# Splitting the expert biases on 128 partitions, and both last out projections ahead of turning and routing

## The reference

```
proj = x @ w_in
  [0:256]      causal pooling, windows 2, 4, 8, 16
  [256:1408]   q, k, v of 6 heads x 64, dilated sliding windows, ALiBi
  [1408:2176]  gate * a -> causal depthwise conv of 31 taps -> LN -> swish
mix = concat(pool, attention, conv) @ w_o
x   = LN(alpha*x + mix)
x   = LN(alpha*x + MoE(x))
MoE: logits = x @ router_w + router_b; top 4 of 32 experts, softmax over the four
     hh = x @ e_w_in[e] + e_b_in[e]; gate, up = split(hh)
     act = min(gate,7) * sigmoid(1.702*gate) * (clip(up,-7,7) + 1)
     y  += gate_weight * (act @ e_w_out[e] + e_b_out[e])
```

## Time and profile before

| | before |
|---|---|
| median of 3 runs | 1374.19 us |
| profiled execution | 1375.13 us, span 1373.2 us |
| mean granted TensorE clock | 0.945 |
| PE, DVE, ACT, POOL busy | 1185.9, 533.3, 272.9, 281.9 us |
| DMA | 463.14 MB, mean 337 GB/s |

### The profile page before, as it was taken

How to read it: one execution, slowest core, us unless ns; L and a number is a source line. 1 busy time by engine, 2 the same in 40 slices (tenths; PEclk the granted TensorE clock), 3 DMA queues, 4 the chain that set the end, 5 groups by cost and what they waited for, 6 DMA issues and landing times.

```text
span 1373.2 us, 34108 instructions
## 1 busy us (share of the span) xinstructions
PE 1185.9 (86%) x12516; PEld 532.6 (39%) x12517; DVE 533.3 (39%) x866; ACT 272.9 (20%) x533; POOL 281.9 (21%) x242
## 2 busy tenths in 40 slices
PE   8688999855899999999989999998998989987860
PEld 7577555431333343343233333342333332532220
DVE  3997846653422231324222222222314220432226
ACT  0001333311102221132121212130121211131123
POOL 5900000222121221112211141023121212130113
PEclk9889999957999999999999999999999999998975
DMA  9700680355999999999999999999999999999953
GB/s 335 219 3 0 240 283 33 123 216 204 417 413 411 412 411 413 415 404 406 415 418 410 415 401 413 410 416 402 415 408 414 410 419 393 392 404 419 410 221 126
DMA packets 78828, 463.14 MB, mean 337 GB/s; under 512 B 11908, under 2 KB 19689, under 8 KB 28493
## 3 DMA queue, kind: packets, MB, share of 16 engines
q1 hardware_dynamic: 67931, 438.16, 78.5%
q0 software_dynamic: 8800, 18.26, 5.2%
q10 hardware_dynamic: 2066, 6.32, 1.3%
HBM read 448.29 MB, written 19.48 MB: 341 GB/s over the span
## 4 chain that ended last, share of the span: by engine, by line
PE 54%; DMA 17%; issue 3%; DVE 2%; ACT 0%; SPq 0%; ACTq 0%; DVEq 0%; POOLq 0%; POOL 0%
PE pu L1812 34%; PE rest L1826 18%; DMA ring<-in_e_in 10%; DMA ring<-in_e_out 7%; PE pu L1806 1%; PE rest L1837 1%; DVE fin L2028 0%; DVE bn L2010 0%; DVE xgT L1949 0%; DVE mv L2021 0%; DMA acc_rows<-y,row 0%; DMA fin<-acc_rows 0%; PE rest L1831 0%; ACT y L1892 0%; DMA xq<-x_rows,idx 0%
## 5 line engine op out<-in xcount | busy, mean ns | idle before, releaser
L1812 PE MATMUL pu<-ring,xgT 128*32 128x512 f32 x5248 | 589.6, 601 | 35.3 <-DMA ring<-in_e_in 34.5
L1812 PEld LDWEIGHTS pu<-ring,xgT 128*32 128x32 f32 x5248 | 168.0, 111 | 439.8 <-issue 432.8
L1826 PE MATMUL rest<-ring,hid 128*32 128x256 f32 x5248 | 299.0, 385 | 16.9 <-DMA ring<-in_e_out 11.7
L1979 DVE TENSOR_SCALAR gg<-pu 128x1280 f32<-128x1280 f32 x32 | 47.7, 1492 | 603.6 <-PE pu L1812 603.6
L1735 POOL DMA_INDIRECT acc_rows<-y,row x82 | 110.3, 1346 | 778.4 <-ACT y L1892 737.6
L1826 PEld LDWEIGHTS rest<-ring,hid 128*32 128x32 f32 x5248 | 168.6, 111 | 137.5 <-issue 35.1
L1892 ACT ACTIVATE y<-rest,gate 32x256 f32 x328 | 153.1, 467 | 287.1 <-issue 275.2
L1872 ACT ACTIVATE ss<-gg 128x1280 f32<-128x1280 f32 x32 | 40.7, 1272 | 544.8 <-DVE gg L1979 544.8
L867 PE MATMUL pair<-xt,ring 128*128 128x260 f32 x448 | 104.2, 396 | 20.4 <-DVE conv L1189 14.9
L867 PEld LDWEIGHTS pair<-xt,ring 128*128 128x128 f32 x448 | 88.3, 198 | 35.2 <-DVE conv L1189 15.7
L1725 POOL DMA_INDIRECT xq<-x_rows,idx x82 | 88.3, 1076 | 58.7 <-issue 46.8
(11 more groups left out here) (263 smaller groups left out, 589.7 us busy)
## 6 DMA issues: line engine op xcount, KB each, us to landing
ring<-in_e_in SPq DMA_DIRECT2D x256, 1024.0 KB, 23.1
ring<-in_e_out SPq DMA_DIRECT2D x128, 1024.0 KB, 24.5
ring<-in_w_in SPq DMA_DIRECT2D x3, 1536.0 KB, 30.0
ring<-in_w_in SPq DMA_DIRECT2D x5, 512.0 KB, 9.2
ring<-in_w_o SPq DMA_DIRECT2D x1, 2048.0 KB, 11.9
conv<-in_x_prompt SPq DMA_DIRECT2D x1, 2048.0 KB, 13.8
x_rows<-conv ACTq DMA_DIRECT2D x4, 512.0 KB
acc_rows<-conv ACTq DMA_DIRECT2D x4, 512.0 KB
```

Of the source, the lines that this page charges most:

```text
L1812: mm = nc.tensor.matmul(pu[quarter(c), j], xgT[:, j, k], w[:, :, c * QC:(c + 1) * QC], start=False, stop=k == KT - 1, skip_group_check=True)
L1826: mm = nc.tensor.matmul(py[quarter(c), j], hid[:, j, 2 * q + f], w[:, f, c * QC:(c + 1) * QC], start=False, stop=q == FT // 2 - 1 and f == ...
L1979: V.tensor_scalar(gg[:, :, :], pu[:, :, 0], SW_LIMIT, None, ALU.min).then_inc(g_ready, 1)
```

## The change

The biases are loaded once. Each of the four column quarters goes to one band of 32 partitions of `btok`, 768 columns wide (512 of gate and up, 256 of the out bias), so that 128 partitions are used. GpSimd casts and subtracts in whole: three casts, two subtractions. The three parts then stand in `parts`, in the place of the values, and 24 transfers of SyncE (4 quarters x 3 parts, one for `brow` and one for `drow` each) bring them to their partitions. The loads no longer wait for the input. SyncE waits for the split ahead of the transfers, ScalarE for the transfers (`bias_rows`) where it waited for `brow_ready`, VectorE for the split alone where it waited for `drow_ready`.

In the attention's end, `ln1(1)` moves from step 11 to step 12 (`NORM_AT`), `turn_rows1(1)` and `logits(1)` from the steps 12 and 13 to behind `out_rest(0)`, and `route(1)` behind `ln1(0)`.

```
-TURN_AT = {3: 6, 2: 9, 1: 12}
-LOGITS_AT = {3: 7, 2: 10, 1: 13}
+TURN_AT = {3: 6, 2: 9}
+LOGITS_AT = {3: 7, 2: 10}
+NORM_AT = {3: 5, 2: 8, 1: 12}
...
-        btok = qkv[:, 6 * R:]
-        otok = mix[:, 6:8, :].rearrange("p a r -> p (a r)")[:, 0:D]
+        btok = mix[:, 6:8, :].rearrange("p a r -> p (a r)")[:, 0:3 * QC]
+        parts = qkv[:, 6 * R:6 * R + 9 * QC // 2].bitcast(BF16).rearrange("p (k n) -> p k n", k=3)
...
+            sp.wait_ge(split_ready, 1)
+            for part in range(3):
+                to = slice(part * NE, (part + 1) * NE)
+                for c in range(NQ):
+                    of = slice(c * NE, (c + 1) * NE)
+                    sp.dma_start(brow[to, c].rearrange("p a n -> p (a n)"), parts[of, part, 0:2 * QC]
+                                 ).then_inc(bias_rows, 16)
+                    sp.dma_start(drow[to, c * QC:(c + 1) * QC], parts[of, part, 2 * QC:]).then_inc(bias_rows, 16)
...
-            gp.wait_ge(ld["xt2"], 16)
+            for c in range(NQ):
+                gp.dma_start(btok[c * NE:(c + 1) * NE, 0:2 * QC].rearrange("p (a n) -> p a n", a=2),
+                             o["e_brow"].rearrange("e (a c n) -> e c a n", a=2, c=NQ)[:, c]).then_inc(ld["brow"], 16)
+            for c in range(NQ):
+                gp.dma_start(btok[c * NE:(c + 1) * NE, 2 * QC:3 * QC], o["e_bout"][0][:, c * QC:(c + 1) * QC]
+                             ).then_inc(ld["bout"], 16)
+            sp_ch = Chain(gp, split)
+            gp.wait_ge(zeroed, 4)
+            nc.gpsimd.memset(brow[3 * NE:, :, :, :], 0.0).then_inc(bias_rows, 1)
+            gp.wait_ge(bias_rows, 1)
+            nc.gpsimd.memset(drow[3 * NE:, :], 0.0).then_inc(bias_rows, 1)
...
             for part in range(3):
...
+                sp_ch.do(nc.gpsimd.tensor_copy(parts[:, part], btok[:, :]))
+                if part < 2:
+                    sp_ch.do(nc.gpsimd.tensor_tensor(btok[:, :], btok[:, :], parts[:, part], ALU.subtract))
+            gp.sem_inc(split_ready, 1)
...
-            a.wait_ge(brow_ready, 1)
+            a.wait_ge(bias_rows, 2 + 16 * 6 * NQ)
...
-            top_exps(1, NTH[1])
+            ln1_root(1, NTH[1])
+            x1_store(1, NTH[1])
+            keep_x1T(1)
             ln1_root(0, NTH[0])
+            top_exps(1, NTH[1])
             keep_x1T(0)
...
             out_rest(0)
+            turn_rows1(1)
+            logits(1)
+            turn_rows1(0)
             rank(1)
-            turn_rows1(0)
             logits(0)
...
-            d.wait_ge(drow_ready, 1)
+            d.wait_ge(split_ready, 1)
...
-            route(1)
             ln1(0)
+            route(1)
             weigh(1, NTH[1])
```

More of the change, by code:

```diff
@@ L192, in attention_steps @@
         turns += [("probs", n - 1)] if 1 <= n <= NSTEPS else []
-    return steps + ["rest0", "rest1"], turns + [("x1", 0)]
+    return steps + ["rest0", "rest1"], turns + [("x1", 1), ("x1", 0)]
 AFTER, TURNS = attention_steps()
@@ L473, in first_block @@
         split = bsem("bias_split_steps")
-        brow_ready = bsem("brow_ready")
+        split_ready = bsem("bias_split_ready")
+        bias_rows = bsem("bias_rows_in_place")
         placed_in_lists = bsem("placed_in_lists")
@@ L601, in _ @@
             sp.wait_ge(copied, 48)
+            sp.wait_ge(bias_rows, 2 + 16 * 6 * NQ)
             sp.wait_ge(k_stored[1], 32)
@@ L615, in _ @@
             nc.gpsimd.memset(chosen4[:, :, :], 0.0).then_inc(zeroed, 1)
-            gp.wait_ge(ld["xt2"], 16)
-            for part in range(3):
-                gp.dma_start(btok[part * NE:(part + 1) * NE], o["e_brow"]).then_inc(ld["brow"], 16)
-            for part in range(3):
-                gp.dma_start(otok[part * NE:(part + 1) * NE], o["e_bout"][0]).then_inc(ld["bout"], 16)
-            gp.wait_ge(zeroed, 4)
-            sp_ch = Chain(gp, split)
-            sp_ch.do(nc.gpsimd.memset(brow[:, :, :, :], 0.0))
@@ L625, in _ @@
-            gp.wait_ge(ld["brow"], 48)
-            by_quarter = lambda lo, hi: btok[lo:hi].rearrange("p (a c n) -> p c a n", a=2, c=NQ)
-            def keep_high(lo, hi):
-                for c in range(NQ):
-                    sp_ch.mark(nc.gpsimd.tensor_copy(brow[lo:hi, c], by_quarter(lo, hi)[:, c]))
-                sp_ch.wait()
-            def take_off(lo, hi):
-                for c in range(NQ):
-                    sp_ch.mark(nc.gpsimd.tensor_tensor(by_quarter(lo, hi)[:, c], by_quarter(lo, hi)[:, c],
-                                                       brow[lo:hi, c], ALU.subtract))
-                sp_ch.wait()
@@ L638, in _ @@
-            keep_high(0, 3 * NE)
-            for part in (1, 2):
-                take_off(part * NE, (part + 1) * NE)
-                keep_high(part * NE, (part + 1) * NE)
-            take_off(2 * NE, 3 * NE)
-            keep_high(2 * NE, 3 * NE)
-            gp.sem_inc(brow_ready, 1)
+            for c in range(NQ):
+                gp.dma_start(btok[c * NE:(c + 1) * NE, 0:2 * QC].rearrange("p (a n) -> p a n", a=2),
+                             o["e_brow"].rearrange("e (a c n) -> e c a n", a=2, c=NQ)[:, c]).then_inc(ld["brow"], 16)
@@ new lines, in _ @@
+            for c in range(NQ):
[6 more added lines that the diff above has]
+            nc.gpsimd.memset(drow[3 * NE:, :], 0.0).then_inc(bias_rows, 1)
+            gp.wait_ge(bias_rows, 2)
@@ L656, in list_rows @@
                         bounds_check=GS * NE * MAXQ - 1, oob_is_err=False).then_inc(listed, 16)
-            gp.wait_ge(ld["bout"], 48)
-            def keep_high_out(lo, hi):
-                sp_ch.do(nc.gpsimd.tensor_copy(drow[lo:hi], otok[lo:hi]))
-            def take_off_out(lo, hi):
-                sp_ch.do(nc.gpsimd.tensor_tensor(otok[lo:hi], otok[lo:hi], drow[lo:hi], ALU.subtract))
-            sp_ch.do(nc.gpsimd.memset(drow[:, :], 0.0))
-            keep_high_out(0, 3 * NE)
-            for part in (1, 2):
-                take_off_out(part * NE, (part + 1) * NE)
-                keep_high_out(part * NE, (part + 1) * NE)
-            take_off_out(2 * NE, 3 * NE)
-            keep_high_out(2 * NE, 3 * NE)
-            gp.sem_inc(drow_ready, 1)
             gp.wait_ge(conv_out, 1)
@@ L819, in _ @@
                     ln1_root(NT, 1)
-                for i in REST_AT:
-                    if n == REST_AT[i]:
+                for i in TURN_AT:
+                    if n == NORM_AT[i]:
                         ln1_root(i, NTH[i])
@@ L835, in _ @@
                     keep_values(n - 2)
+            ln1_root(1, NTH[1])
+            x1_store(1, NTH[1])
+            keep_x1T(1)
+            ln1_root(0, NTH[0])
             top_exps(1, NTH[1])
-            ln1_root(0, NTH[0])
             keep_x1T(0)
@@ L1492, in _ @@
                     place_in_lists(NT, 1, ranks_of(NT))
-                for i in REST_AT:
-                    if n == REST_AT[i]:
+                for i in NORM_AT:
+                    if n == NORM_AT[i]:
                         ln1(i)
@@ L1503, in _ @@
                     row_norms(n)
+            ln1(0)
             route(1)
-            ln1(0)
             weigh(1, NTH[1])
```

3 lines of the change are left out of this document (2 added, 1 removed).

## The result

The changed kernel takes 1355.78 us (median of 4 runs, 1354.28 to 1357.11) beside 1374.51 us for the kernel before on the same chip: ratio 0.9864, 95% interval 0.9849 to 0.9878, so 18.7 us are saved where 31.6 were forecast. The time lies 6 us above the end of my range. The profiled execution took 1357.11 us (span 1355.2), where the kernel before had a span of 1373.2.

The account below looks back on a forecast made before the run. It took the fixed-length expert weight stream as the bound, its start set by the first block. Savings of 18.2 us before and 13.4 us at attention's end, 31.6 in all, gave a median of 1342.6 us, range 1339 to 1346.5.

Parts of the forecast that it names:

- the expert stage is a block of fixed length: Expert stage: DMA-bound with fixed duration, so every microsecond saved in the first block comes off the end, one for one.
- after the last logits all is the same chain: From last logits to the end: nothing changes, unit loads issue 11 to 14 us earlier, so the 13.4 us saving passes through.
- list of what would prove it wrong: Early taps still 1.3 us, ScalarE waiting for placed rows, over 4 us between tile 0's rows and logits, longer expert stage.
- Taps and GpSimd: VectorE's convolution: taps are slowed by GpSimd's bias split; without it 0.75 us each from the first, convolution done 19.1 us earlier.
- taps slow for another reason: Rival, convolution: DMA traffic slowed the taps, so only 4.6 us return there, with the tail 18: 1356 us; chance 0.02.
- Loads of the bias: Kernel start: 384 KB of bias share the DMA engines with input and first weights, delaying TensorE's start 0.8 us (0 to 1.0).
- Split: GpSimd, before the taps: three casts and two subtractions take 8.1 us, end at 20 to 22 us, cost VectorE nothing.
- 24 transfers: SyncE, between key cache and mask: 24 issues at 0.35 us, 8.4 us, mask out at 51 to 53 us, cost nothing.
- Tail: End of attention: last out projection starts earlier and takes 5.42 us, fewer waits for normalised rows; 13.4 us saved.
- The sum: Whole kernel: 18.2 us up to the last attention pair plus 13.4 us at attention's end, 31.6 us saved.
- The rivals of 1348 to 1356: Attention's end gives only 8 us: 1348, chance 0.08; up to taps slowed by DMA traffic: 1356, chance 0.02.

Follow-up runs that it names:

- with 29: Changed kernel plus 29 increments of an unused semaphore on GpSimd, between the bias split and its wait for the convolution: 1344.40 us, ratio 0.9779.
- the tail alone: Kernel before with only the edit of the attention's end, bias split and loads as before: 1360.90 us, ratio 0.9904.

## Why the prediction was wrong, and where it was right

- **The step that failed** is the first one, a term that the sum put at nothing: "the expert stage is a block of fixed length", with "after the last logits all is the same chain". I held it for all kernels with the same stream, and costed an edit of GpSimd's code by what its instructions do, not by where it leaves those behind it. The measured price is 6.5 us inside the stage and 4.2 us at the exit. The prediction's list of what would prove it wrong ends with a longer expert stage, but no rival had it. With the length restored the forecast is nearly met: 1344.4 and 1343.8 us against 1342.6, inside the range.
- **Taps and GpSimd: right.** 752 ns from the first tap (0.75 forecast). That "taps slow for another reason" was wrong is shown by the same DMA share at full speed. (By the earlier trace rows the four taps end at 65.27 + 6.16 = 71.43, not 71.35, and 2.8 below 1342.6 is 1339.8, not 1339; neither changes the forecast.)
- **Loads of the bias: mis-sized.** I put 0.8 us (0 to 1.0) on TensorE's start. The first gate product came at 25.50 instead of 22.00, 3.5 us (2.2 to 4.6 in the executions above), since the 384 KB delayed the weights and the input: TensorE waits 1.83 us for weights between its 8th and 9th matmul, and with 29 it waits 1.68 us for the input at 13.35. The run with the loads behind the input gave 3.9 back. My sum took their bytes at the full rate; why they cost more than that, no run separates. So the means gained 15.8, not 18.2.
- **Split: right, even early.** Five instructions in 6.0 us, over at 18.1 (8.1 us and 20 to 22 forecast). The prices by columns were the right ones.
- **24 transfers: right in cost, wrong in size.** An issue took 0.59 and not 0.35 us, with the mask at 54.73; ScalarE's first value copy stood at 131.32 and did not wait for them.
- **Tail: right.** 13.1 us against 13.4; the last projection took the 5.42 us, tile 0's turn waited 2.32 us, and the tail alone measured 13.2.
- **The sum.** 28.8 at the last logits and 0.5 at the hand-over make the 29.3 us of the stream's start; less 6.5, 4.2 and 0.5 behind the final loads, 18.1, beside the 18.0 of the spans. The rivals of 1348 to 1356 would have given a time like the measured one, for reasons that the runs exclude.

## What to carry to other kernels

An edit ahead of a runtime loop can change the price of the loop: here 29 instructions fewer raised the packets of the instruction queue from 13 to 40, and 29 idle ones took both the packets and 11.4 us back. So compare these packets in the profile, before and after, and if they have risen, pad with idle instructions until they fall back. Look at it first when all work is where it was and only gaps marked "issue" have grown. And in a stage like this one, with the DMA share at 1.01, count single-row transfers by the time of their packets, one behind the other, not by their bytes: 24 rows of 8 KB cost the stage 12.6 us whole and 1.3 us in 16 pieces each.

## What was not expected of the hardware

- 29 idle instructions on GpSimd gave 11.4 us (1355.78 to 1344.40), and 99 cost the kernel before 10.9 us by the ratio.
- GpSimd's fetches were 8 KB packets of 0.31 us inside the stage, from 520 to 1300 us 20, five in each turn of its loop, in the slow placements and none in the fast ones. 29 and 157 instructions of padding, 128 apart, took 1344.40 and 1343.75 us, 93, between them, 1356.15.
- A transfer of one row was one packet of data where it went from or to SBUF (62 rows of 4 KB: 62 packets of 4 KB, 11.2 us of stage; 24 rows of 8 KB: 24 packets of 8 KB, 12.6 us), and 16 packets of 512 B from HBM to HBM (31 rows of 8 KB: 0.3 us).
- A gather 7 us late, three units ahead of its use, cost nothing in five turns (stage 1015.24 us, 1015.58 without the delay).
